# Neighbourhood attention: a running minimum in place of maximum and negation, score pieces of 288, the mask in four parts

## What is computed

```python
def row_block(args):                     # one row of 64 queries, 8 heads of 64
    r, q_row = args
    r0 = jnp.clip(r - kh // 2, 0, rows - kh)
    k_rows = lax.dynamic_slice_in_dim(kg, r0, kh, axis=1)    # kh = 8 rows of the 16 x 64 grid
    ...
    sc = jnp.einsum('bjqhd,bkjchd->bhjqkc', qb, k_band) * scale
    sc = jnp.where(mask, sc + bias, -jnp.inf)                # position bias, column mask
    p = jax.nn.softmax(sc, axis=(-2, -1))
    o = jnp.einsum('bhjqkc,bkjchd->bjqhd', p, v_band)
```

## Time and profile before

| | us |
|---|---|
| three runs | 2635.86, 2635.47, 2630.23 |
| median | 2635.47 |
| profiled execution | 2633.64 |
| its span in the trace | 2631.9 |
| TensorE busy | 2564.0 (97%) |
| VectorE busy | 1383.3 (53%) |
| ScalarE busy | 895.2 (34%) |
| GpSimd busy | 282.8 (11%) |
| load share of 16 DMA engines | 29.8% |

### The profile page before, as it was taken

The page is one execution under the profiler, slowest core; times in us unless marked ns, Lnnn a source line. Parts: engine busy times, 40 slices in busy tenths (PEclk is TensorE's granted clock), DMA queues, the critical chain, the costliest instruction groups (busy, mean ns, idle before and its releaser), DMA issues.

```text
span 2631.9 us, 33408 instructions
## 1 busy us (share of the span) xinstructions
PE 2564.0 (97%) x12000; PEld 2086.5 (79%) x12000; DVE 1383.3 (53%) x2136; ACT 895.2 (34%) x1394; POOL 282.8 (11%) x275
## 2 busy tenths in 40 slices
PE   8999999999999999999999999999999999998998
PEld 4578888888887888888888888888778897886677
DVE  5864555555545443454444444444551224998873
ACT  2432222222223322242222222222322125887751
POOL 1200000000002000100000000000010002557631
PEclk9899999999999999999999999999999999999999
DMA  8532232323212710331102111100334464345521
GB/s 293 192 112 80 81 112 80 112 80 111 68 61 81 192 44 0 112 101 44 64 32 64 34 62 37 59 32 1 112 118 107 144 162 98 97 108 148 159 71 64
DMA packets 178576, 245.18 MB, mean 93 GB/s; under 512 B 55856, under 2 KB 132784, under 8 KB 178480
## 3 DMA queue, kind: packets, MB, share of 16 engines
q1 hardware_dynamic: 178480, 243.92, 29.8%
HBM read 210.33 MB, written 39.58 MB: 95 GB/s over the span
## 4 chain that ended last, share of the span: by engine, by line
PE 89%; DVE 5%; issue 3%; POOL 2%; ACT 1%; DMA 0%; DVEq 0%; POOLq 0%; SPq 0%; ACTq 0%
PE banks L1876 24%; PE banks L1878 24%; PE banks L1877 24%; PE banks L2332 3%; PE banks L2314 2%; PE banks L1966 2%; PE banks L2302 1%; PE banks L2301 1%; PE banks L1907 1%; PE banks L2133 1%; PE banks L2134 1%; PE banks L2135 1%; DVE Hlo L1533 1%; DVE acc L1361 1%; PE banks L2284 1%
## 5 line engine op out<-in xcount | busy, mean ns | idle before, releaser
L1876 PE MATMUL banks<-Hhi,Whi 128*128 128x512 f32 x1696 | 670.2, 395 | 6.9 <-ACT TB L1140 5.2
L1877 PE MATMUL banks<-Hlo,Whi 128*128 128x512 f32 x1696 | 663.7, 391 | 0.0
L1878 PE MATMUL banks<-Hhi,Wlo 128*128 128x512 f32 x1696 | 663.6, 391 | 0.0
L1576 DVE SCALAR_TENSOR_TENSOR X<-banks,mod,X 128x512 f32<-128x512 f32 x512 | 380.9, 749 | 207.0 <-PE banks L1878 204.2
L1876 PE MATMUL banks<-Mhi,Whi 128*128 128x512 f32 x1024 | 400.0, 391 | 0.0
L1878 PE MATMUL banks<-Mhi,Wlo 128*128 128x512 f32 x1024 | 398.5, 389 | 0.0
L1877 PE MATMUL banks<-Mlo,Whi 128*128 128x512 f32 x1024 | 398.4, 389 | 0.0
L1876 PEld LDWEIGHTS banks<-Hhi,Whi 128*128 128x128 f32 x1696 | 321.4, 189 | 77.6 <-ACT TB L1140 6.0
L1877 PEld LDWEIGHTS banks<-Hlo,Whi 128*128 128x128 f32 x1696 | 320.8, 189 | 68.1 <-issue 2.2
L1878 PEld LDWEIGHTS banks<-Hhi,Wlo 128*128 128x128 f32 x1696 | 320.5, 189 | 67.6
L1008 ACT ACTIVATE Whi<-stage 128x2048 fp32r<-128x2048 f32 x89 | 169.8, 1908 | 541.0 <-PE banks L1878 541.0
(11 more groups left out here) (203 smaller groups left out, 2828.6 us busy)
## 6 DMA issues: line engine op xcount, KB each, us to landing
stage<-w SPq DMA_DIRECT2D x64, 1024.0 KB, 5.5
stage<-ada_w SPq DMA_DIRECT2D x48, 1024.0 KB, 5.3
stage<-w_in SPq DMA_DIRECT2D x13, 1024.0 KB, 6.8
stage<-sgu_in SPq DMA_DIRECT2D x8, 1024.0 KB, 7.1
x_saved<-X SPq DMA_DIRECT2D x16, 512.0 KB, 2.6
QS<-q_heads SPq DMA_DIRECT2D x32, 256.0 KB, 4.2
KH<-k_heads SPq DMA_DIRECT2D x32, 256.0 KB, 5.3
KL<-k_heads SPq DMA_DIRECT2D x32, 256.0 KB, 6.1
```

Source lines behind the costliest of these rows:

```text
L1576: nc.vector.scalar_tensor_tensor(out=X[:, k, half(hf)], in0=Dn[:, i % D_BANKS, :], scalar=gate[:, k:k + 1], in1=X[:, k, half(hf)], op0=ALU ...
L1876: nc.tensor.matmul(out_bank, whi, xhi, start=start, stop=False)
L1877: nc.tensor.matmul(out_bank, whi, xlo, start=False, stop=False)
L1878: return nc.tensor.matmul(out_bank, wlo, xhi, start=False, stop=stop)
```

## The change

Four edits, all in kind B:

- the add instruction now computes -(scores + bias) and the running minimum of that, which is the negated maximum, straight into `neg_max`. The separate negation is gone, with the semaphore `bias_added` between them; those who waited for it wait for `max_done`. The exponential reads the negated scores with a scale of -1;
- 576 score columns are computed as two pieces of 288, each in a bank of its own, in place of 512 and 64;
- the mask is added in four parts of 368 columns;
- the parts stand in steps 3, 5, 6 and 7 for the second head, and 11, 13, 14 and 15 for the next pair's first. These steps have no gating. The first part carries the wait for the bias load, as before.

```diff
+MASK_PARTS = 4
     def masked(self, e):
-        v = (self.n["v"] // PAIR - 4) * 4 + 2 * e + 2
-        return self.reg * 4 + v if self.reg is not None else v
+        v = ((self.n["v"] // PAIR - 4) * 2 + e + 1) * MASK_PARTS
+        return self.reg * 2 * MASK_PARTS + v if self.reg is not None else v
...
+    def piece(n):
+        return H if n % H == 0 else n // 2
...
-            reach(eng, bias_added, T.b_units(QT * (e - 1) + PAIR * ahead))
+            reach(eng, max_done, T("v", QT * (e - 1) + PAIR * ahead))
...
-                at = slice(part * (NF + NI) // 2, (part + 1) * (NF + NI) // 2)
+                at = slice(part * (NF + NI) // MASK_PARTS, (part + 1) * (NF + NI) // MASK_PARTS)
...
-                    if kind == "B" and u in (5, 6):
-                        mask_bias(T, 1, u - 5)
-                    if (kind == "B") != last and u in (13, 14):
-                        mask_bias(T, 0, u - 13, ahead=1)
+                    if kind == "B" and u in (3, 5, 6, 7):
+                        mask_bias(T, 1, (3, 5, 6, 7).index(u))
+                    if (kind == "B") != last and u in (11, 13, 14, 15):
+                        mask_bias(T, 0, (11, 13, 14, 15).index(u), ahead=1)
...
                 nc.scalar.activation(PE_[:, u % 2, 0:n], scores, ACT.Exp, bias=neg_max[:, u % 4:u % 4 + 1],
+                                     scale=-1.0 if kind == "B" else 1.0,
...
-                    scores = SC[:, u % 2, 0:n]
-                    bank = SB_[:, 2 * (u % 2):2 * (u % 2) + 2, :].rearrange("p b n -> p (b n)")[:, 0:n]
+                    m = piece(n)
+                    scores = SC[:, u % 2, 0:n].rearrange("p (b n) -> p b n", n=m)
+                    bank = SB_[:, 2 * (u % 2):2 * (u % 2) + n // m, 0:m]
                     nc.vector.memset(top_score[:, 1:2], 0.0)
-                    nc.vector.tensor_tensor_reduce(out=scores, in0=bank, in1=bias[u // QT % 2][:, b0:b0 + n], scale=1.0,
-                                                   scalar=-3e38, op0=ALU.add, op1=ALU.max,
-                                                   accum_out=top_score[:, 0:1]).then_inc(bias_added, 1)
-                    dve.wait_ge(bias_added, T.b_units(u + 1))
-                    nc.vector.tensor_scalar(out=neg_max[:, at:at + 1], in0=top_score[:, 0:1], scalar1=-1.0,
-                                            scalar2=None, op0=ALU.mult).then_inc(max_done, 1)
+                    nc.vector.tensor_tensor_reduce(out=scores, in0=bank, in1=bias[u // QT % 2][:, b0:b0 + n].rearrange("p (b n) -> p b n", n=m), scale=-1.0,
+                                                   scalar=3e38, op0=ALU.add, op1=ALU.min,
+                                                   accum_out=neg_max[:, at:at + 1]).then_inc(max_done, 1)
...
                 if (kind if u >= 2 else before) == "B":
-                    pe.wait_ge(bias_added, T.b_units(u - 1))
+                    pe.wait_ge(max_done, T("v", u - 1))
...
-                for at in range(0, n, H):
-                    m = min(H, n - at)
-                    bank = SB_[:, 2 * (u % 2) + at // H, 0:m]
+                m = piece(n)
+                for at in range(0, n, m):
+                    bank = SB_[:, 2 * (u % 2) + at // m, 0:m]
```

More of the change, by code:

```diff
@@ L93, in add @@
             self.n[name] += k
-    def b_units(self, u):
-        return self("v", u - 4 * PAIR)
     def masked(self, e):
-        v = (self.n["v"] // PAIR - 4) * 4 + 2 * e + 2
-        return self.reg * 4 + v if self.reg is not None else v
+        v = ((self.n["v"] // PAIR - 4) * 2 + e + 1) * MASK_PARTS
+        return self.reg * 2 * MASK_PARTS + v if self.reg is not None else v
     def loads(self, n, first=0, ahead=0):
@@ L371, in build @@
     bias_loaded = [sem(f"bias_loaded{i}") for i in range(2)]
-    bias_masked, mask_loaded, bias_added = sem("bias_masked"), sem("mask_loaded"), sem("bias_added")
+    bias_masked, mask_loaded = sem("bias_masked"), sem("mask_loaded")
     s_ready, max_done, exp_done = sem("s_ready"), sem("max_done"), sem("exp_done")
```

## The result

The changed kernel takes 2651.0 us (median of 4 runs, 2648.17 to 2651.92), the kernel before 2634.5 beside it: ratio 1.0061, 95% interval 1.0049 to 1.0074. It is 16.5 us slower, 0.6%. The prediction had the direction and most of the mechanism, and less than half of the size: 2642.5, with a range that ends at 2648.

The account below looks back on a forecast made before the run. Bound: a VectorE-ScalarE ring of 2.13 us a step, a second ring through GpSimd close behind. Terms 7.3+1.9-1.2-1.0 = +7.0 us; with the runs' median of 2635.47 before, 2642.5 us, range 2632 to 2648.

Parts of the forecast that it names:

- The negation, the pieces, the semaphores: Neighbourhood attention: dropping the negation gains 0.7 us a head; pieces of 288 cost and gain nothing; semaphores delay nothing.
- Before the first wait: Stretch ahead of the first costly mask wait, where smaller mask parts hold scales less: -1.0 us.
- The new period: Query load to next query load, with GpSimd waiting for the bias: 18.9 us a head, +7.3 us over five.
- from query load to landing: A head's query load issue to its bias landing: 11.3 us, the mean of five loads before.
- from landing to the next query load: Wake, mask part and the GpSimd chain up to the next head's query load: 7.6 us.
- The last pair: Last neighbourhood pair: a sixth wait in step 3 costs +1.9 us, the remaining eleven steps gain 1.2.
- the 0.2 us of room: Slack of the second ring, through GpSimd: copy ends at 2445.89, exponential starts at 2446.09.
- The rule on the write receipt: A load's semaphore fires only after the last byte is confirmed; this receipt is most of about 2 us fixed cost.
- A: Rival: GpSimd's own room absorbs the bias wait and the gains remain: -7.8 us, 2627.7; chance 0.18.
- B: Rival: six bias waits cost 1.1 us each instead of 2.1: +1 us, 2636.5, no change; chance 0.2.
- C: Rival: gating pushed into the next mask adds 0.5 us per wait, +3, 2645.5; within the 0.62 for slower.
- D: Rival: the copy releases the exponential, not the negation; costs the forecast 1 us, 2643.5; within the 0.62 for slower.

Follow-up runs that it names:

- x8: Changed kernel, with the second head's value load moved behind the next bias load in the first three pairs: 2648.1 us, ratio 1.0052 to the kernel before.
- x2: Changed kernel, with the bias load issued ahead of the same head's query and key loads: 2627.5 us, ratio 0.9974 to the kernel before.
- x6: Kernel before, with the minimum of negated scores replacing maximum and negation, nothing else: 2630.3 us beside 2634.3, ratio 0.9987.

## Why the prediction was wrong

**Which mechanism:** right in the main. The mask's early part waits for a load that did not move with it, and the wait goes to all engines. There are seven waits: 0.43 us for the first pair's step 3, hidden as predicted (the scale behind that mask waits 0.54 us more for its reciprocal), and 3.3 to 4.9 for the other six (predicted 2.5 to 4). The query loads, forecast 18.5 to 19.5 us apart in the middle pairs, are 20.3 to 22.5 apart. What the mechanism lacked is TensorE's clock, below.

**The negation, the pieces, the semaphores:** right. Forecast 5.6 us for 8 heads at 0.7; measured 4.0 alone and 5.2 with the pieces, which their intervals do not tell apart. The pieces: none, measured none. 0.756 us for the add-and-minimum against 0.76, 0.97 for the mask part against 0.98.

**Before the first wait:** right. The first query load comes 1.0 us later in the trace after, but the first neighbourhood reciprocal is 1.9 late already, from stages that the change does not touch; within the part it is 0.9 sooner, and I said 1.0.

**The new period:** here the sum failed. I took 11.3 + 7.6 = 18.9 us a head. The five stretches from 2397.27 to 2499.42 sum to 102.15 us, 87.13 before: +15.0 where I had +7.3. Two terms were mis-sized or incomplete, and together they are the whole 7.7:
- "from query load to landing", taken from five loads before as 11.3, is 12.0 on average (60.1 in sum for 56.5): +3.6. I treated the landing as a fixed delay. The change moved the loads closer together, which may be why it is not (x8); that stays open. My range allowed 0.5 us a wait; it took 0.7.
- "from landing to the next query load", 7.6, is 8.4 in the changed kernel: +4.1 over five. With the clock held it is 7.60, so the chain was right and TensorE's clock was missing. I had written that TensorE would be idle more "with the same work", and did not ask what an idle TensorE does to the clock. There was reason to ask: a clock of 1.00 with TensorE busy 45 of 50 us is all that the earlier trace rows shows, and the longest gap of TensorE in this part of the kernel before was 1.6 us, so no row of it showed what the clock does behind one of 2 to 4.

**The last pair:** +0.7 forecast (1.9-1.2); from its query load to the first reciprocal behind its sixteen steps (2518.64 before, 2537.35 after) it is 37.9 us for 35.2, +2.7. Its landing is 12.2 us for 11.5, and its clock falls too. The terms of this last pair that the prediction names, 0.7 and 0.3, add to 1.0 and not to its 1.2; that is no part of the miss.

**The account.** In the traces the part is 0.9 shorter up to the first query load, 15.0 longer over five stretches and 2.7 longer in the last pair: +16.8, beside 16.5 between the medians. The forecast had -1.0, +7.3 and +0.7.

**Two readings.** The prediction has the exponential at 2446.09 waiting behind the copy. The copy had ended at 2445.89, and the row puts the wait down to the negated maximum; the 0.2 us of room is the difference, and stands. The rule on the write receipt that it takes from the Trainium skill (DMA: Bandwidth & Descriptors) stands there in the section on loads that GpSimd issues, while these are SyncE's; no term of the sum uses it. In windows of 0.2 us the last traffic of that load lies between 2441.40 and 2441.60, so 0.6 to 0.8 us pass before its landing.

**The rivals.** A, the wait absorbed, is excluded as a reading of the changed kernel, but its price fits a kernel without the wait: -7.8 us forecast, -7.8 measured in x2, where the interval goes from -4.5 to -9.5, so the last digit is luck. B, the wait half as dear, fell. C had the direction and 3 of the 8.5 us that were missing, by gating that is pushed into the next mask; with the clock held the stretch is the forecast's 7.6, so that plays no part. D, an exponential that the copy releases anyway, fell: the negation alone gains 4.0 us (x6). The range was too narrow: it allowed 0.5 us a wait for the landing and 0.2 for the chain behind it, and they took 0.7 and 0.8.

## What to carry to other kernels

Before work is moved to an earlier step, follow every wait it carries back to its issue and its landing; a wait that never showed can be near to showing; here the nearest landing was 1.3 us ahead of its mask (2425.49 and 2426.76). Here the cure cost nothing: the load that is needed first goes first in its queue, and the same edit that lost 16 us wins 8 (x2). And when a stall leaves TensorE idle for some microseconds, add what follows at half clock to its price: here 0.8 us of each head came back when TensorE was merely kept busy, 3.4 of 16.5 us by the medians.

## What the runs showed of the hardware

Behind the six waits TensorE's gaps are 2.2, 3.2, 4.1, 3.6, 3.1 and 3.8 us. The first left the granted clock at 1.00; windows of 10 us over the other five have it at 0.83, 0.66, 0.83, 0.83 and 0.83 on average, which at the level of 0.50 is 3.4 us each and 6.8 in the third. With 14 dummy matmuls in each gap the clock stayed at 1.00 in all of them, though GpSimd's waits were as long (3.4 to 5.8 us). The length of the gap alone does not tell whether the clock falls: with the mask edit alone it fell behind a gap of 2.16 us (at 2491.72), in x8 it stayed at 1.00 behind one of 2.18 us (at 2491.22). A bias load of 736 KB landed between 6.9 and 9.8 us after its issue over the runs with the same queue ahead of it.
